# Phase rounds, clock products and a weight split moved in the state space stage of a two-layer network

## The reference, cut to what matters

```python
for i in range(DEPTH):
    mod = c_act @ w_ada[i] + b_ada[i]            # six rows of 1024: sh1, sc1, g1, sh2, sc2, g2
    h = modulate(rms_norm(x, norm_g[i, 0]), sh1, sc1)
    h = s5_mixer(...) if i % 2 == 0 else mla_mixer(...)
    x = x + g1 * rms_norm(h, norm_g[i, 1])
    h = modulate(rms_norm(x, norm_g[i, 2]), sh2, sc2)
    h = dense_swiglu(...) if i % 2 == 0 else moe_swiglu(...)
    x = x + g2 * rms_norm(h, norm_g[i, 3])
```

```python
ab = exp(a * dt);  bb = f * b                    # complex, per group and state
h[t] = ab * h[t-1] + bb @ u[t]                   # an associative scan in the reference
y[t] = Re(c @ h[t]) + d * u[t]
z = gelu(y);  gl = z @ w_glu;  out = gl[:, :D] * sigmoid(gl[:, D:])
```

## Time and profile before

| | us |
|---|---|
| median of 3 runs (lowest, highest) | 1039.05 (1038.18, 1040.37) |
| the profiled execution | 1038.83 |
| its span | 1036.9 |
| TensorE busy | 957.9 (92%) |
| VectorE busy | 855.3 (82%) |
| ScalarE busy | 635.1 (61%) |

### The profile page before, as it was taken

The page is one execution under the profiler, slowest core; times in us unless marked ns, Lnnn a source line. Parts: engine busy times, 40 slices in busy tenths (PEclk is TensorE's granted clock), DMA queues, the critical chain, the costliest instruction groups (busy, mean ns, idle before and its releaser), DMA issues.

```text
span 1036.9 us, 16695 instructions
## 1 busy us (share of the span) xinstructions
PE 957.9 (92%) x6354; PEld 800.8 (77%) x6355; DVE 855.3 (82%) x1119; ACT 635.1 (61%) x787; POOL 55.6 (5%) x116
## 2 busy tenths in 40 slices
PE   0685799899999999999999999999999999999995
PEld 0464588899999979767888888888888888888884
DVE  7989985498777856995778998989989898998994
ACT  4436274544433445774477868778686786867762
POOL 4002300010000001001000000000000000000000
PEclk9987899999999999999899999999999999999998
DMA  9897694699989759602479999999999999999961
GB/s 240 333 344 187 140 324 142 240 341 353 315 275 314 276 188 353 210 34 78 148 264 356 333 397 313 377 376 327 401 316 384 364 337 389 314 387 347 356 248 63
DMA packets 134242, 297.64 MB, mean 287 GB/s; under 512 B 9494, under 2 KB 40843, under 8 KB 133915
## 3 DMA queue, kind: packets, MB, share of 16 engines
q1 hardware_dynamic: 126026, 282.92, 76.1%
q0 software_dynamic: 4080, 8.48, 3.0%
q10 hardware_dynamic: 4064, 5.26, 1.8%
HBM read 291.06 MB, written 3.16 MB: 284 GB/s over the span
## 4 chain that ended last, share of the span: by engine, by line
PE 82%; DVE 13%; ACT 3%; issue 1%; DMA 1%; ACTq 0%; SPq 0%; DVEq 0%
PE ps L643 24%; PE ps L645 24%; PE ps L644 24%; PE ps L1183 1%; PE ps L727 1%; PE ps L1042 1%; PE ps L1156 1%; PE ps L1157 1%; ACT s_low_turned L1444 1%; DVE s_out_map L1943 1%; PE ps L1134 1%; PE ps L744 1%; DMA mod_rows<-ada_wide 0%; DVE s_g L2001 0%; PE ps L1051 0%
## 5 line engine op out<-in xcount | busy, mean ns | idle before, releaser
L2332 DVE TENSOR_TENSOR w_lo<-raw,w_hi 128x2048 fp32r<-128x2048 f32 x162 | 365.7, 2288 | 36.5 <-ACT w_hi L1637 36.5
L1637 ACT ACTIVATE w_hi<-raw 128x2048 fp32r<-128x2048 f32 x162 | 303.0, 1913 | 0.0
L643 PE MATMUL ps<-w_hi,xe_hi 128*128 128x512 f32 x448 | 177.6, 396 | 1.3 <-DVE xe_lo L2292 1.3
L645 PE MATMUL ps<-w_hi,xe_lo 128*128 128x512 f32 x448 | 175.3, 391 | 0.0
L644 PE MATMUL ps<-w_lo,xe_hi 128*128 128x512 f32 x448 | 174.6, 390 | 0.0
L1736 DVE TENSOR_TENSOR w_lo<-raw,w_hi 128x2048 fp32r<-128x2048 f32 (+3 forms) x59 | 131.6, 2249 | 28.8 <-ACT w_hi L1308 27.8
L1308 ACT ACTIVATE w_hi<-raw 128x2048 fp32r<-128x2048 f32 (+3 forms) x59 | 108.7, 1874 | 11.1 <-DMA raw<-in_mla_w_in 6.2
L643 PE MATMUL ps<-act_hi,w_hi 128*128 128x256 f32 x352 | 100.5, 286 | 1.9 <-DVE act_lo L1904 1.9
L645 PE MATMUL ps<-act_hi,w_lo 128*128 128x256 f32 x352 | 99.6, 283 | 0.0
L644 PE MATMUL ps<-act_lo,w_hi 128*128 128x256 f32 x352 | 99.6, 283 | 0.0
L643 PEld LDWEIGHTS ps<-w_hi,xe_hi 128*128 128x128 f32 x448 | 84.2, 188 | 18.3 <-issue 1.5
(11 more groups left out here) (430 smaller groups left out, 1563.3 us busy)
## 6 DMA issues: line engine op xcount, KB each, us to landing
raw<-in_moe_w_in SPq DMA_DIRECT2D x112, 1024.0 KB, 6.9
raw<-in_moe_w_out SPq DMA_DIRECT2D x56, 1024.0 KB, 8.0
raw<-in_w_ada SPq DMA_DIRECT2D x48, 1024.0 KB, 7.7
raw<-in_ffn_w_in SPq DMA_DIRECT2D x44, 512.0 KB, 6.7
raw<-in_ffn_w_out SPq DMA_DIRECT2D x11, 1024.0 KB, 7.7
raw<-in_ssm_w_glu SPq DMA_DIRECT2D x16, 512.0 KB, 7.4
raw<-in_mla_w_o SPq DMA_DIRECT2D x4, 1024.0 KB, 8.6
raw<-in_mla_w_uq SPq DMA_DIRECT2D x3, 768.0 KB, 7.2
```

The costliest lines, as they stand in the source:

```text
L643: mm(dst, st[0], mv[0], start=first, stop=False)
L645: return mm(dst, st[1], mv[0], start=False, stop=last)
L1637: af(HI[:, (V_MOE + m) % RING, :], RAW[:, (RAW_OF_W[V_MOE] + m) % RING, :], cp).then_inc(hi_done, 1)
L2332: tt_(LO[:, slot, :], RAW[:, (RAW_OF_W[V_MOE] + m) % RING, :], HI[:, slot, :].bitcast(F32), ALU.subtract)\
```

## The change

Three things are done. VectorE: the first three phase rounds go from behind the r_blocks to between `mod_rows(0)` and `mod_rows(1)`. TensorE: `keep_warm(20, 6)` is put ahead of `strips(0)`, another one ahead of `strips(1)` (with a wait for the copies of the first strip, whose bank it writes), and `keep_warm(8, 7)` ahead of the state products of half 0; the wait `strip_ok` 4 moves up with it. VectorE again: the split of weight unit 0 goes from between the two skip terms to behind the second one and behind `z_lo(0)`.

```diff
--- before.py
+++ after.py
@@ -821,6 +821,9 @@
                                 last = mm(y_tile(g), U[:, g, :], chunk_map(g),
                                           start=False, stop=False)
                 last.then_inc(y_ps, 1)
+                if hf == 0:
+                    pe.wait_ge(strip_ok, 4)
+                    keep_warm(8, 7)
                 pe.wait_ge(s_ok, 2 * hf + 2)
                 for dt in dts:
                     for a in range(2):
@@ -867,11 +870,13 @@
             state_inputs(1)
             for n in range(15, 20):
                 ada(n)
+            keep_warm(20, 6)
             strips(0)
             mod_columns(3)
+            pe.wait_ge(strip_ok, 2)
+            keep_warm(20, 6)
             strips(1)
             outputs(0)
-            pe.wait_ge(strip_ok, 4)
             keep_warm(8, 7)
             outputs(1)
             mod_columns(4)
@@ -1949,7 +1954,20 @@
             norm_rows(0, XN0, XN0)
             for r in range(1, 6):
                 r_block(r)
+            def phase_rounds(k0, k1):
+
+                for k in range(k0, k1):
+                    m = 1 << k
+                    z = [TURN[:, 0, 3 + k, :], TURN[:, 0, k - 1, :]] if k else [sm(17), sm(15)]
+                    y = [a.unsqueeze(2).broadcast_to([P, GI, m]) for a in z]
+                    link_(cmul([TAB[:, c, :, m:2 * m] for c in range(2)], [TAB[:, c, :, 0:m] for c in range(2)], y, tmp(m)))
+
             mod_rows(0)
+            dve.wait_ge(rblk_ok, 12)
+            v_.memset(TAB[:, 0, :, 0:1], 1.0)
+            link_(v_.memset(TAB[:, 1, :, 0:1], 0.0))
+            dve.wait_ge(fun_ok, 3)
+            phase_rounds(0, 3)
             mod_rows(1)
             mod_columns(0)
             mod_columns(1)
@@ -1957,14 +1975,7 @@
                 r_block(r)
 
             dve.wait_ge(rblk_ok, 16)
-            v_.memset(TAB[:, 0, :, 0:1], 1.0)
-            link_(v_.memset(TAB[:, 1, :, 0:1], 0.0))
-            dve.wait_ge(fun_ok, 3)
-            for k in range(5):
-                m = 1 << k
-                z = [TURN[:, 0, 3 + k, :], TURN[:, 0, k - 1, :]] if k else [sm(17), sm(15)]
-                y = [a.unsqueeze(2).broadcast_to([P, GI, m]) for a in z]
-                link_(cmul([TAB[:, c, :, m:2 * m] for c in range(2)], [TAB[:, c, :, 0:m] for c in range(2)], y, tmp(m)))
+            phase_rounds(3, 5)
             v_.memset(R8T[:, :, 0:1], 0.0)
             v_.tensor_copy(R8T[:, :, 1:], sm(20).unsqueeze(2).broadcast_to([P, GI, NJ - 1])).then_inc(tab_ok, 1)
             dve.wait_ge(tab_ok, 1)
@@ -2029,11 +2040,12 @@
 
             dve.wait_ge(y_ps, 2)
             skip_term(0)
-            split_to(1)
             mod_rows(4)
             dve.wait_ge(y_ps, 4)
             skip_term(1)
-            for n in range(4):
+            z_lo(0)
+            split_to(1)
+            for n in range(1, 4):
                 z_lo(n)
             split_to(2)
             mod_columns(4)
```

## The result

| | before | changed |
|---|---|---|
| median of 13 runs, us | 1038.56 | 1041.64 |
| lowest, highest | 1037.81, 1040.37 | 1039.54, 1048.90 |
| the profiled execution | 1038.83 | 1044.18 |
| its span | 1036.9 | 1042.2 |

The changed kernel is slower: the ratio to the kernel before is 1.0032, with a 95% interval of 1.0021 to 1.0043, so 2.2 to 4.5 us. Its runs scatter over 9 us where those of before scatter over 2.6. The profiled execution is 2.5 us above the median of its kernel, so sizes read from it can be larger than in most runs.

What follows compares the result with a forecast made beforehand. It took the first GLU matmul, set by VectorE's length, to decide, with fixed TensorE matmul time behind it. Start -0.6 and clock +1.2 gave +0.6 us on 1038.83 (profiled) or 1039.05 (median); it said 1039.5, range 1037.1 to 1041.7.

Steps and rivals of the forecast that it cites:

- Part 2: Twenty clock products ahead of strips(0): they end at 91.8, and only 0.5 us of the 2.5 us gain remains.
- Part 4: Both halves ahead of the moved split: first GLU matmul at 131.6 against 132.19, -0.6 us; skip_term(1) keeps 1.4 us slack.
- Part 1: Phase rounds in VectorE's old wait: VectorE gains 2.5 us from round 3, second modulation row 1.2 us late.
- rival (d): State inputs or ada over 1.2 us late, strips(0) delayed one for one by the twenty products: 1041 to 1042, chance 0.07.
- Part 3: Products ahead of strips(1) and of the states: both hidden, the new eight by 0.3 us, ending at 111.4.
- rival (c): Added products at half clock from strips(1) on, last state product late for skip_term(1) at 125.45: 1041.2, chance 0.12.
- Part 5: Clock at the GLU's start: 3.5 us TensorE idle, then 3 to 5 us at half clock, net +1.2 us.

Runs made afterwards that it cites:

- e11: Kernel before with only the three phase rounds moved, timed a second time: 1036.92 us, ratio 0.9974.
- e1: Kernel before with only the three phase rounds moved, first timing: 1036.90 us, ratio 0.9993.
- e9: Kernel before with the phase rounds moved and only the later 20 and 8 added products, split in its old place: 1037.96 us, ratio 0.9987.
- e3: Kernel before with only the split of weight unit 0 moved: 1041.30 us, ratio 1.0021.
- e5: Kernel before with the split moved and 21 keep-warm products in place of nine ahead of the GLU: 1038.57 us, ratio 0.9997.
- e6: Kernel before without the nine keep-warm products ahead of the GLU, split in its old place: 1040.27 us, ratio 1.0018.
- e10: Kernel before with the phase rounds moved and only the first 20 added products, split in its old place: 1039.50 us, ratio 1.0002.
- e4: Changed kernel without the twenty keep-warm products ahead of strips(0): 1041.71 us, ratio 1.0025 to the kernel before.
- e7: Changed kernel without any added products, so phase rounds and split moved: 1040.43 us, ratio 1.0022 to the kernel before.
- e12: Changed kernel with 21 keep-warm products in place of nine ahead of the GLU: 1040.35 us, ratio 1.0027 to the kernel before.

## Why the prediction was wrong

The forecast was +0.5 us and no change that can be measured; the time, 1041.64, is at the upper edge of the range, and the kernel is slower by more than its interval. In the profile the GLU begins at 134.88, where the forecast had 131.6. Of these 3.3 us, 1.8 are Part 2 and 1.4 are the wait that Part 4 had at nothing. By the steps:

**Part 1** was right: 3.67 us of rounds in the wait, 1.2 to 1.5 us of delay for the row (the second column is at 57.70, 1.5 later), 2.2 us earlier at round 3, first turned block at 76.26 against 76.0. Alone it is worth 1.7 to 3.8 us by e11, while e1, with two runs near 1044, allows for nothing.

**Part 2 failed in size, and with it the sign.** "They end at 91.8" rested on ada products at full clock, with the reason that "TensorE runs at full clock without a break there". The clock was full there in the one trace of before; in twelve of the thirteen traces of the other kernels (all but e9) the clock is at half over part of 75 to 87 us, also in those where this stretch of the program is as before (e3, e5, e6). In the changed kernel it fell among the small state inputs, and they took 1.7 us more for it. The ada products end at 88.9 and not at 87.2, the clock products at 93.5, and o_high(3) comes at 100.50 and not at 98.7. Instead of a gain of 0.5 the term was a loss of 1.3 in that trace, and 2.9 us against the rounds alone in e10. This is rival (d): the state inputs or ada more than 1.2 us late, each microsecond lost one for one, 1041 to 1042. It had 0.07.

**Part 3** called the later twenty and the new eight hidden. In the changed kernel's trace the twenty are, with 0.73 us to spare, but the new eight begin when the state is ready and hold the state products back by 1.9 us, on the chain that ended last. They were to begin at 109.5 and began at 113.4, since the strip's DMAs came late and the chunk products ran at half clock. e9 against e11 puts the later 28 near 1 us, with intervals that overlap.

**Part 4 failed where it gave skip_term(1) a slack of 1.4 us.** I let the last state product come at 124.0. It came at 126.3 in e3, 127.0 in e4, 128.6 in e7 and 128.7 in the changed kernel. The step took TensorE to be waiting for VectorE's state, with all its products at full clock and the strip's DMAs 2 us early. The changed kernel's trace shows TensorE with work up to the end from 110.15 on: chunk products at half clock (3.28 us for 1.96), the new eight, a stop of 1.69 us, and the old eight at half clock (3.47 us for 2.05). The rival (c) named this wait and its point, 125.45, but gave it 0.12. This step is also why the gain of Part 1 doesn't come back when the first twenty are taken out (e4, 1041.71): what VectorE wins ahead of the second skip term it then waits there.

**Part 5 had the mechanism and too small a size.** The clock fell ahead of the first matmul as expected, and stayed at half on the GLU for 5 to 6 us in the changed kernel and in e3, not 3 to 5, for 3 us in e6 and e7, and not at all in e4. In the changed kernel's profile 2.0 us more than before were lost, against the +1.2 of the sum, and 2.2 to 2.7 us in the times of e3. The sum was also low by its own working: 3 to 5 us at half are 1.5 to 2.5 us lost, not 1.1 to 2.5. (Part 4's terms add up to 9.67 and not 9.65, which changes nothing.)

By the Trainium skill, page "TensorE: Matmul & The Clock Gate", section "Why this matters for your kernels", an idle gap between bursts of matmuls costs the full rate. The traces of e3 and e6, with gaps of 3.45 and 3.05 us and 0.50 behind them, agree; that of e4, with a gap of 3.46 us and 1.00 behind it, does not.

Put together by ratios, rounds 0.9974, first twenty +0.0028, later products +0.0013, split +0.0021 give 1.0036, near the 1.0032 measured. That they meet is luck: in e4 the first twenty are gone and the loss is not, since the wait of Part 4 takes their place, and in e12 the cold start is gone and the ratio hardly moves. What is shown is that the first twenty cost 2.9 us on top of the rounds (e10 against e11), that the half clock behind the moved split costs 2.5 us (e3 against e5), and that either one takes the whole gain of the rounds away (e10, e7). How the loss of the changed kernel divides among the causes is not shown, and products with the split but without the rounds were not run.

## What to carry to other kernels

Products that keep the clock up are real work in an engine's program: put them where the engine waits in every run, behind the work that others wait for, and size them by the half clock too; here twenty of them ahead of a strip turned 2.5 us of lead into idle time of VectorE. Work moved from a covered place to the last one before a matmul burst makes an idle time there: 3.45 us of it cost 2.2 us behind it in e3, and twelve more products in the gap took that away. When several changes meet at one start, take each alone and in pairs: here the rounds alone were a gain, and the rounds with either of the others a loss. And one profile gives one course of the clock: before a term rests on "at full clock", look at what the term is at half.

## What was not expected of the hardware

The clock fell to half while TensorE was busy: in the changed kernel over 78.5 to 84 us, 5.50 of 5.50 us busy, granted 0.53. What ran before and in it were state inputs (64 columns of weights, 32 of data) and modulation products with 32 weight columns; so a busy engine in the profile is no guarantee of the full level. A stop of 1.41 us ended at 77.04, 1.7 us before the fall; the trace of before has a stop of 1.36 us at that place and no fall, and no run takes the stop and the small products apart.

The same idle time did not do the same in each execution: 3.45 us ahead of the GLU were followed by 5 to 6 us at half in the changed kernel and in e3, by 3 in e7, and 3.46 us by none in e4.

And stops in TensorE's stream that have no releaser, of 0.2 to 4.0 us each, 1 to 7 us in total between 60 and 140 us, stand at other places in each kernel (about 1.4 us in the state inputs in several, 3.97 in the zero products of e4, 1.69 in the states of the changed kernel). What they are was not tried.
